# Opening of a two-layer transformer trunk: order of products and transfers, and unread products in TensorE's gaps

## The reference

```
def rms_norm(x, g):
    y = xf * lax.rsqrt(jnp.mean(xf * xf, axis=-1, keepdims=True) + NORM_EPS)
    return (y * g)
def modulate(xn, shift, scale):
    return xn * (1 + scale) + shift
def ffn_sublayer(x, g, shift, scale, gate, w_in, w_out):
    return x + FFN_RES * gate * swiglu(modulate(rms_norm(x, g), shift, scale), w_in, w_out)
...
mx = jnp.split((silu_c @ w_mod[i] + b_mod[i])[:, None, :], N_MOD, axis=-1)
mc = jnp.split((silu_cc @ w_mod[i] + b_mod[i])[None, None, :], N_MOD, axis=-1)
x = ffn_sublayer(x, g_norm[i, 0], mx[0], mx[1], mx[2], ffn_w_in[i, 0], ffn_w_out[i, 0])
```

## Time and profile before

| what | value |
|---|---|
| median of 3 runs | 1694.1 us (1694.03 to 1694.1) |
| profiled execution, its time | 1694.78 us |
| profiled execution, its span | 1692.9 us |
| TensorE busy | 1658.0 us, 98% of the span |
| VectorE, ScalarE busy | 1131.6 us, 599.9 us |
| mean granted TensorE clock | 0.994 of full |
| chain that ended last, TensorE's share | 91% |

### The profile page before, as it was taken

How to read it: one execution, slowest core, us unless ns; L and a number is a source line. 1 busy time by engine, 2 the same in 40 slices (tenths; PEclk the granted TensorE clock), 3 DMA queues, 4 the chain that set the end, 5 groups by cost and what they waited for, 6 DMA issues and landing times.

```text
span 1692.9 us, 23695 instructions
## 1 busy us (share of the span) xinstructions
PE 1658.0 (98%) x8903; PEld 1413.2 (83%) x8903; DVE 1131.6 (67%) x1876; ACT 599.9 (35%) x810; POOL 129.9 (8%) x80
## 2 busy tenths in 40 slices
PE   8999999999999899999999999999999999999998
PEld 6788888889777798888888898888888987889997
DVE  5877778778575678787787773463333687576665
ACT  3321222234676533212212342222212455443443
POOL 0000000000786100000000000000000022000000
PEclk8999999999999999999999999999999999999999
DMA  8755555542211035555555422432222231055552
GB/s 300 279 206 185 188 189 192 200 162 75 100 51 51 25 133 195 189 191 200 198 186 198 150 75 99 174 124 99 99 97 87 91 131 69 21 176 198 190 198 76
DMA packets 45426, 247.45 MB, mean 146 GB/s; under 512 B 5168, under 2 KB 5296, under 8 KB 25008
## 3 DMA queue, kind: packets, MB, share of 16 engines
q1 hardware_dynamic: 45360, 246.55, 40.4%
HBM read 245.48 MB, written 1.05 MB: 146 GB/s over the span
## 4 chain that ended last, share of the span: by engine, by line
PE 91%; DVE 6%; ACT 1%; issue 1%; DMA 0%; SPq 0%; POOL 0%; ACTq 0%; DVEq 0%
PE ps L1796 13%; PE ps L1798 13%; PE ps L1805 13%; PE ps L1627 10%; PE ps L1628 10%; PE ps L1629 10%; PE ps L2258 5%; PE ps L1654 4%; PE ps L1961 3%; PE ps L2264 2%; PE ps L1911 1%; PE ps L2062 1%; PE ps L1992 1%; PE ps L1834 1%; DVE w_lo L1204 1%
## 5 line engine op out<-in xcount | busy, mean ns | idle before, releaser
L1796 PE MATMUL ps<-a_hi,w_hi 128*128 128x512 f32 x960 | 374.1, 390 | 0.8 <-ACT w_hi L679 0.8
L1798 PE MATMUL ps<-a_lo,w_hi 128*128 128x512 f32 x960 | 373.8, 389 | 0.0
L1204 DVE TENSOR_TENSOR w_lo<-raw,w_hi 128x2048 fp32r<-128x2048 f32 x114 | 260.5, 2288 | 49.7 <-ACT w_hi L679 21.7
L1627 PE MATMUL ps<-h_hi,w_lo 128*128 128x512 f32 (+1 forms) x648 | 235.0, 363 | 1.5 <-POOL h_lo L569 1.4
L1629 PE MATMUL ps<-h_hi,w_hi 128*128 128x512 f32 (+1 forms) x648 | 233.6, 360 | 0.0
L1628 PE MATMUL ps<-h_lo,w_hi 128*128 128x512 f32 (+1 forms) x648 | 233.6, 360 | 0.0
L1805 PE MATMUL ps<-a_hi,w_lo 128*128 128x512 f32 x960 | 227.4, 389 | 0.0
L1796 PEld LDWEIGHTS ps<-a_hi,w_hi 128*128 128x128 f32 x960 | 180.2, 188 | 38.9 <-issue 0.8
L1805 PEld LDWEIGHTS ps<-a_hi,w_lo 128*128 128x128 f32 x960 | 180.2, 188 | 37.4
L1798 PEld LDWEIGHTS ps<-a_lo,w_hi 128*128 128x128 f32 x960 | 180.2, 188 | 37.3
L673 ACT ACTIVATE work<-ps 128x512 f32<-128x512 f32 x66 | 39.4, 598 | 431.6 <-PE ps L1805 419.1
(11 more groups left out here) (331 smaller groups left out, 2529.5 us busy)
## 6 DMA issues: line engine op xcount, KB each, us to landing
raw<-wstream SPq DMA_DIRECT2D x147, 1024.0 KB, 4.9
mring<-wmod SPq DMA_DIRECT2D x144, 512.0 KB, 3.5
spare<-wstream SPq DMA_DIRECT2D x11, 1024.0 KB, 4.8
xT<-tokens SPq DMA_DIRECT2D x4, 512.0 KB, 5.8
cb<-cond SPq DMA_DIRECT2D x1, 1024.0 KB, 7.8
out<-mring SPq DMA_DIRECT2D x4, 256.0 KB, 2.1
mring<-gain SPq DMA_DIRECT2D x1, 512.0 KB, 6.2
cst<-consts SPq DMA_DIRECT2D x1, 449.0 KB, 7.2
```

The source lines that it names most:

```text
L1204: dve.tensor_tensor(w_lo[:, slot], raw[:, slot], w_hi[:, slot].bitcast(F32), ALU.subtract).then_inc(lo_ready, 1)
L1627: pe.matmul(dst, lhs_lo, rhs_hi, start=start, stop=False, skip_group_check=True)
L1796: pe.matmul(bank, hi, a_hi[:, k, 0:nt], start=k == 0, stop=False, skip_group_check=True)
L1798: pe.matmul(bank, hi, a_lo[:, k, 0:nt], start=False, stop=False, skip_group_check=True)
```

## The change

Edits in five places, all in the opening:

1. TensorE runs 20 unread products at the start instead of 12, three more between each two column sums, three behind chunk 0, five behind turn 0, one behind chunk 1 and three behind turn 1.
2. The spread of the root stands ahead of turn 0. Tile 0's units with slab 0 stand ahead of chunk 1, and tile 0's units with slab 1 ahead of chunk 2; the part 2 units of tiles 0, 1 and 2 come later.
3. VectorE writes tile 0's low part ahead of the copy of chunk 1, splits slab 0 and slab 1 in passes 2 and 3 instead of 1 and 2, and moves three small steps behind the copy or behind all passes.
4. ScalarE splits slab 1 ahead of tile 1 instead of tile 2, and copies identity and mask after all tiles.
5. SP issues the first token tiles ahead of the conditioning columns, modulation tiles 0 and 1 ahead of the tables, and only identity and selector of `cst` there; the rest (384 KB) follows behind tile 15.

```diff
-WARM = 12
+WARM, WARM_GAP = 20, 3
...
-            sp.dma_start(ccol[:], cond_cols).then_inc(in_cond, 16)
             for n in range(4):
                 k = slice(2 * n, 2 * (n + 1))
                 sp.dma_start(xT[:, k], tokens[:, k]).then_inc(in_tok[n], 16)
-            sp.dma_start(cst[:], consts).then_inc(in_small, 16)
-            sp.dma_start(vec[:], vecs).then_inc(in_small, 16)
+                if n == 0:
+                    sp.dma_start(ccol[:], cond_cols).then_inc(in_cond, 16)
             for n in range(MOD_FIRST):
                 mod_tile(n, n % 4, n - 3 if n >= 4 else None)
+                if n == 1:
+                    sp.dma_start(cst[:, 0:C_MASK], consts[:, 0:C_MASK]).then_inc(in_small, 16)
+                    sp.dma_start(vec[:], vecs).then_inc(in_small, 16)
                 if n in (1, 3):
                     slab(n // 2, n // 2)
+            sp.dma_start(cst[:, C_MASK:N_CONST], consts[:, C_MASK:N_CONST]).then_inc(in_tables, 16)
...
             split_hi(0, 0, 0)
             for k in range(DT):
-                if k == 2:
+                if k == 1:
                     split_hi(1, 1, 1)
...
             for k in range(DT):
+                if k == 1:
+                    first_low(0)
                 dve.wait_ge(mod_dots, 2 * k + 2)
                 dve.tensor_copy(mod_rows_sb[:, half(k % 2)], ps[MOD_BANK[k % 2]][:, 0:LAT]).then_inc(mod_rows, 1)
                 if k == 0:
+                    dve.wait_ge(in_small, 32)
+                    link(dve.tensor_scalar(bscale[:], vec[:, V_BMOD + DT:V_BMOD + 2 * DT], 1.0, None, ALU.add))
                     dve.wait_ge(rstd_bc, CALL["ffn0"] + 1)
-                else:
+                elif k > 1:
                     first_low(k - 1)
                 first_scaled(k)
-                if 1 <= k < 3:
-                    split_lo(k - 1, k - 1)
+                if 2 <= k < 4:
+                    split_lo(k - 2, k - 2)
...
+            unread_products(WARM)
             for k in range(0, DT, 2):
+                if k:
+                    unread_products(WARM_GAP)
                 pe.wait_ge(ss_sum, k + 2)
...
             mod_chunk(0)
+            unread_products(WARM_GAP)
             pe.wait_ge(in_small, 32)
+            token_spread(CALL["ffn0"], NORM_BANK, 0, 4)
             turn_chunk(0)
-            token_spread(CALL["ffn0"], NORM_BANK, 0, 4)
+            unread_products(5)
+            first_products(0, 0, (0, 1))
             for m in range(1, DT):
+                if m == 2:
+                    first_products(1, 0, (0, 1))
                 mod_chunk(m)
-                if m >= 2:
+                if m == 1:
+                    unread_products(1)
+                if m >= 3:
                     first_products(1, m - 2, (0, 1))
                 turn_chunk(m)
-                first_products(0, m - 1, (0, 1) if m == 1 else (0, 1, 2))
-                if m == 2:
+                if m == 1:
+                    unread_products(3)
+                else:
+                    first_products(0, m - 1, (0, 1) if m < 4 else (0, 1, 2))
+                if m == 3:
                     first_products(0, 0, (2,))
+                    first_products(0, 1, (2,))
+                if m == 4:
+                    first_products(0, 2, (2,))
```

More of the change, by code:

```diff
@@ L98 @@
 N_VEC = V_WDW + CT * TAPS
-C_ID, C_MASK, C_COS, C_SIN = 0, P, 3 * P, 3 * P + LAT
-C_SEL = C_SIN + LAT
-N_CONST = C_SEL + 2
+C_ID, C_SEL = 0, P
+C_MASK = C_SEL + 2
+C_COS = C_MASK + 2 * P
+C_SIN = C_COS + LAT
+N_CONST = C_SIN + LAT
 COLT = 32
@@ L220, in build @@
         in_small = sem("in_small")
+        in_tables = sem("in_tables")
         raw_loaded = [sem(f"raw_loaded{i}") for i in range(3)]
@@ L739, in _ @@
                 act.activation(first_sq(k), xT[:, k], ACT.Square).then_inc(sq_ready, 1)
-            act.wait_ge(in_small, 32)
-            act.activation(ident_r[:], ident, ACT.Copy).then_inc(act_const, 1)
-            act.activation(mask_r[:], cst[:, C_MASK:C_MASK + 2 * P].rearrange("p (a n) -> p a n", a=2),
-                           ACT.Copy).then_inc(act_const, 1)
             split_hi(0, 0, 0)
             for k in range(DT):
-                if k == 2:
+                if k == 1:
                     split_hi(1, 1, 1)
@@ L751, in _ @@
                                    bias=shift[:, 0, v, k:k + 1]).then_inc(nhi_ready, 1)
+            act.wait_ge(in_small, 32)
+            act.activation(ident_r[:], ident, ACT.Copy).then_inc(act_const, 1)
+            act.wait_ge(in_tables, 16)
+            act.activation(mask_r[:], cst[:, C_MASK:C_MASK + 2 * P].rearrange("p (a n) -> p a n", a=2),
+                           ACT.Copy).then_inc(act_const, 1)
             act.wait_ge(in_rows, 16)
@@ L1400, in _ @@
             rsqrt(CALL["ffn0"], ps[NORM_BANK][:, 0:4], 0, 1.0 / D, NORM_EPS)
-            dve.wait_ge(in_small, 32)
-            link(dve.tensor_scalar(bscale[:], vec[:, V_BMOD + DT:V_BMOD + 2 * DT], 1.0, None, ALU.add))
-            link(dve.tensor_scalar(nsink[:], vec[:, V_SINK:V_SINK + HEADS], -1.0, None, ALU.mult))
-            link(dve.tensor_scalar(vec[:, V_WDW:N_VEC], vec[:, V_WDW:N_VEC], 0.5, None, ALU.mult))
             for k in range(DT):
+                if k == 1:
+                    first_low(0)
                 dve.wait_ge(mod_dots, 2 * k + 2)
@@ L1408, in _ @@
                 if k == 0:
+                    dve.wait_ge(in_small, 32)
+                    link(dve.tensor_scalar(bscale[:], vec[:, V_BMOD + DT:V_BMOD + 2 * DT], 1.0, None, ALU.add))
                     dve.wait_ge(rstd_bc, CALL["ffn0"] + 1)
-                else:
+                elif k > 1:
                     first_low(k - 1)
                 first_scaled(k)
-                if 1 <= k < 3:
-                    split_lo(k - 1, k - 1)
+                if 2 <= k < 4:
+                    split_lo(k - 2, k - 2)
             first_low(DT - 1)
+            link(dve.tensor_scalar(nsink[:], vec[:, V_SINK:V_SINK + HEADS], -1.0, None, ALU.mult))
+            link(dve.tensor_scalar(vec[:, V_WDW:N_VEC], vec[:, V_WDW:N_VEC], 0.5, None, ALU.mult))
             n0 = ffn(0, TOK, lambda s, w, b: both_tail(s, "ab", w, b), MOD_FIRST, ((0, 0, ("gate",)), (0, 1)))
@@ L1914, in first_products, with unread_products @@
                     last.then_inc(slab_done, 1)
-            for n in range(WARM):
-                pe.matmul(ps[7][:, 0:P], ones[:], ones[:], start=True, stop=True)
+            def unread_products(n):
+                for _ in range(n):
+                    pe.matmul(ps[7][:, 0:P], ones[:], ones[:], start=True, stop=True)
+            unread_products(WARM)
             for k in range(0, DT, 2):
+                if k:
+                    unread_products(WARM_GAP)
                 pe.wait_ge(ss_sum, k + 2)
@@ L2402, in _constants @@
     sel = np.tile(np.eye(COLT)[:, 0:2], (P // COLT, 1))
-    c = np.concatenate([np.eye(P), mask0, mask1, np.tile(cos, (2, 1)), np.tile(sin, (2, 1)), sel], axis=1)
+    c = np.concatenate([np.eye(P), sel, mask0, mask1, np.tile(cos, (2, 1)), np.tile(sin, (2, 1))], axis=1)
     return np.ascontiguousarray(c, dtype=np.float32)
```

## The result

The changed kernel has a median of 1698.08 us (1692.1 to 1700.65, 20 runs) against 1694.1 (1692.6 to 1698.31, 20 runs) for the kernel of before, timed beside it. The medians are 4.0 apart. The ratio, which weighs all the times and not only the middle ones, is 1.0017 with a 95% interval of 1.0009 to 1.0025, so 2.9 us more (1.5 to 4.2). The forecast was 1693.0, with a range to 1696.8. The median lies outside it, on the side of rival 1.

The account below looks back on a forecast made before the run. TensorE was taken to bound the kernel, running without pause from 27.44 us, so only earlier time could be gained. Forecast: 1692.9 - 1.1 + 1.88 - 0.68 = 1693.0 us, range 1691.3 to 1696.8.

Parts of the forecast that it names:

- rival 1: Three products between column sums are too thin; clock falls at about 12.5, returns at 22.75; +2.6 us against before, chance 0.16.
- VectorE's last pair of squares is ready by 11.6, so TensorE alone sets this: Column sums: VectorE's squares arrive early enough that TensorE's work alone sets their end, 13.9 instead of 14.4, 0.5 us gained.
- The wait for it at 27.4 is gone: TensorE's wait for slab 1: slab ready at 22.3, before TensorE asks at 23.3.
- a bound of 23.25: Slab 1's split: ready at 23.25 if the new transfer order saves nothing, second tile's high part 0.3 later.
- The price by bytes of the large pieces: Slab 1's landing: 0.38 MB of tables moved from in front, at 0.41 MB per us some 0.95 us earlier.
- Opening products until 8.0: Start of TensorE: 20 unread products run until 8.0, so column sums start there instead of 7.83, 0.2 us lost.
- Sums done and the root started at 13.9: End of the column sums: at full clock they finish at 13.9 instead of 14.4, and the root chain starts then.
- waits before turns 2 and 3: TensorE idle 0.5 us before turn 2 and 1.2 us before turn 3, the latter released by VectorE's split.
- none before turn 4: TensorE before turn 4: 0.3 us idle was forecast, waiting for VectorE's copy of chunk 4.
- the silu of the broadcast vectors fitted: ScalarE near 51.19: two table copies, 0.7 us, fit ahead of this silu within a wait of 1.0.
- chunks 0 and 2 never waited for a tile: Modulation tiles in the opening: chunk 0 or 2 waiting for its tile was listed as a sign of a wrong forecast.
- the sum of 1.1 us: Whole opening: chunk 5 starts 1.26 us earlier, less 0.2 for walk error, so 1.1 us gained; forecast chance 0.70.

Follow-up runs that it names:

- e5: Changed kernel with the conditioning columns issued ahead of the token tiles again, other transfers in the new order; 1694.06 us against 1694.25 before, ratio 0.9995.
- e6: Changed kernel with the old transfer order, except the conditioning columns stand behind the first token transfer; 1696.26 us against 1694.25 before, ratio 1.0017.
- e11: Kernel of before with only the conditioning columns moved behind the first token transfer; 1696.08 us against 1694.05 before, ratio 1.0011.
- e12: Changed kernel itself, timed a second time on another chip; 1693.6 us against 1694.05 before, ratio 1.0004.
- e13: Changed kernel itself, timed a third time on another chip; 1694.65 us against 1694.38 before, ratio 1.0009.
- e1: Changed kernel with the whole old order of transfers put back; 1694.67 us against 1694.48 before, ratio 1.0001.
- e8: Changed kernel with nine unread products instead of three between the first and second column sums; 1695.35 us against 1694.25 before, ratio 1.0008.
- e9: Changed kernel with the conditioning columns behind all four token transfers and their silu behind the squares; 1693.33 us against 1694.05 before, ratio 0.9997.
- e10: Changed kernel with columns first, 18 opening unread products, and two in each sums gap and behind chunk 0; 1696.05 us against 1694.05 before, ratio 1.0008.
- e16: Changed kernel with the conditioning columns behind all four token transfers, profiled once; 1691.93 us, one time.
- e14: Changed kernel with the conditioning columns behind all four token transfers, timed again on another chip; 1693.11 us against 1694.38 before, ratio 0.9992.
- e15: Changed kernel itself, profiled once more; 1698.5 us, one time.

## Why the prediction was wrong, and where it was right

**The step that failed** is the sentence "VectorE's last pair of squares is ready by 11.6, so TensorE alone sets this". It took the landing of the tokens from the old order of transfers. I priced the new order for the modulation tiles and for slab 1, by bytes standing in front of them, and did not price it for the tokens themselves, since nothing but 8 KB had been put among them. By bytes that is nothing. The runs show 1.3 us on the second token tile (e5 against e6), 0.9 in the old kernel (e11 against before), or a wait of 1.4 to 1.5 for the third (e12, e13). Where it was the second, VectorE's last pair was ready at 13.2 instead of 11.6, an idle stretch of 1.2 opened that the unread products were to close, and the clock fell behind it; the root started at 17.3 instead of 13.9.

**A second term failed with it.** "The wait for it at 27.4 is gone" holds for the profiled execution only because everything else was late there. The forecast had slab 1 landed at 20.4 and split at 22.3, with a bound of 23.25 if the order saves nothing. In the changed kernel at full clock it landed at 22.4 and was split at 24.3, and TensorE waited 0.81 and 0.74 for it (e12, e13). The same small transfer goes with it: the slab lands at 20.98 in e5, which differs from the changed kernel by the place of the columns alone. The price by bytes of the large pieces did come true: in e1, with the tables back in front, slab 1 lands at 21.91, 0.93 later than in e5, where I had 0.95. What bytes did not price is the 8 KB.

**Rival 1** had the right event (the clock falls once in the middle of the sums and returns near 22) and not the right cause. It blamed the thinness of three products; e8, and e5 and e9 with three in every gap, show that three are enough where no idle stretch comes to it; whether two are, e10 leaves open. Its price was 2.6 over before; the profiled opening came to 4.0, of which the late tokens are 1.4 (second pair at 9.76 instead of 8.34). Its chance of 0.16 was too low: 12 of the first 20 executions had a mean clock of .995 or less, and 17 of all 44. The evidence was in the rows. The old kernel's clock had fallen after one idle stretch of 1.5 us, so the whole forecast hung on no such stretch coming back. I should have asked what else could open one.

**Point by point.** Opening products until 8.0: the first sums started at 7.56 in the profile and at 7.25 to 8.8 in the others with 20, as the rise of the clock came earlier or later. Sums done and the root started at 13.9: 17.3 in the profile, 13.5 to 13.7 in e12, e13 and e16, which had full clock. The walk from there on was right in kind. In the profile of e16, which has the forecast's conditions, TensorE's stretch 8 to 12 and its waits before turns 2 and 3 (line 1901):

```profile
8.00:12.00 4.00, 4.00 (x39) 1.00 1.05 412
```
```profile
26.26 0.61 PE L1901 MATMUL ps<-cst,ss 128*128 128x2 f32 x4 [0.55 <-DVE ss L1411]
...
30.82 0.61 PE L1901 MATMUL ps<-cst,ss 128*128 128x2 f32 x4 [0.79 <-DVE ss L1411]
```

The waits are 0.55 where I had 0.5, 0.79 where I had 1.2, and none before turn 4 where I had 0.3. Slab 2's first product is at 56.98; the forecast was 58.04 - 1.1 = 56.94. The wait for slab 1 was gone there, the silu of the broadcast vectors fitted (ScalarE still waited 0.49 for the bank in the changed kernel), and chunks 0 and 2 never waited for a tile. So the sum of 1.1 us holds at full clock for e16's order of transfers (e9 and e14 have 56.88 and 56.48). It does not hold for the changed kernel: at full clock that one gained 0.2 and 0.3 (57.84 and 57.77 in e12 and e13), since it waits for slab 1.

That four executions of the changed kernel took 1692.1 to 1693.2, around the 1693.0 of the forecast, is in part luck. The 1693.0 was counted down from a median of 1694.1 that has the late stretches in it, and the kernel before also has executions at 1692.6 and 1692.7. Fastest against fastest the changed kernel gains 0.5 there, and 0.4 and 0.7 beside e12 and e13; the columns behind the tokens gain 1.0 and 1.2 (e9, e14).

**Spread.** The range was built on three runs of 1694.03 to 1694.1. The kernel before goes from 1692.6 to 1698.3 in 20. Half clock stretches near 1420 and 1490 to 1500 us come in some executions and not in others, and cost about 1.5 each (the distance of 4.1 became 5.6). The profiled execution of before had one of them in plain sight (a granted clock of 0.94 over 1400 to 1425 us); I read only the opening.

**What stays open.** Why the small transfer costs its neighbour 1.3 us, and what decides whether this is the second or the third tile, no run here shows. Why e1's median is no lower than that of before, with a shorter opening at full clock in its profile, is not settled either; with late stretches of 1.5 coming and going, 11 runs do not resolve 0.7. What makes the late stretches is open as well.

## What to carry to other kernels

A fill of unread work only holds the clock as long as nothing else opens a hole behind it, so price the transfers that feed the filled stretch as carefully as the fill. A tiny transfer between large ones that someone waits for was not free here: try it ahead of them, or behind them all, and see what lands when. And take the spread from the clock rows of the whole span before three runs that agree are trusted, and judge an opening by the time at which it ends, not by the whole.

## What the runs showed of the hardware that was not expected

- An 8 KB transfer of 128 rows of 64 bytes, issued as the second of five between four of 512 KB, went with a rate of 293 instead of 388 GB/s in the stretch 4 to 8 us (e6, e5), and one of the large ones landed 1.3 us later. In all nine profiles with it in second place that rate is 277 to 340, in all nine with it first or last 376 to 394.
- TensorE's clock fell from 2.4 to 1.2 GHz at 11.7 us, behind 1.2 us of idle time between column sums (changed kernel), and at 13.1 behind 0.34 in e15; with the same sums and more unread products in place of the wait (e8) it stayed at 2.4.
- The clock rises at another time in each execution: the 20 unread products of the opening ended between 7.4 us (e6) and 8.9 us (e8), with the same products on TensorE up to there.
